# Four feed-forward blocks by a 2x2 block scheme with seven products, in a two-model transformer kernel

## The reference

```python
def _swiglu(x, wg, wu, wd):                    # x (512, 1024); wg, wu (1024, 2816); wd (2816, 1024)
    return (jax.nn.silu(x @ wg) * (x @ wu)) @ wd

for l in range(DEPTH):
    h = 0.5 * _swiglu(x, ffn_w_gate[l, 0], ffn_w_up[l, 0], ffn_w_down[l, 0])
    x = _layernorm(ALPHA * x + h, ln_g[l, 0], ln_b[l, 0])
    h = _mixer(x, ...)
    x = _layernorm(ALPHA * x + h, ln_g[l, 1], ln_b[l, 1])
    h = 0.5 * _swiglu(x, ffn_w_gate[l, 1], ffn_w_up[l, 1], ffn_w_down[l, 1])
    x = _layernorm(ALPHA * x + h, ln_g[l, 2], ln_b[l, 2])
mod = silu(c) @ ada_w + ada_b                  # of the second model, for two vectors c; (1024, 6144)
```

## Time and profile before

| | us |
|---|---|
| median of 3 runs | 3927.68 |
| lowest, highest | 3924.68, 3927.8 |
| span of the profiled execution, first to last instruction | 3922.3 |
| PE busy | 3598.9 (92%) |
| DVE busy | 911.5 (23%) |
| ACT busy | 562.4 (14%) |
| POOL busy | 324.9 (8%) |
| HBM read | 445.96 MB, 115 GB/s over the span |

### The profile page before, as it was taken

How to read it: one execution, slowest core, us unless ns; L and a number is a source line. 1 busy time by engine, 2 the same in 40 slices (tenths; PEclk the granted TensorE clock), 3 DMA queues, 4 the chain that set the end, 5 groups by cost and what they waited for, 6 DMA issues and landing times. The chain is left out here.

```text
span 3922.3 us, 30766 instructions
## 1 busy us (share of the span) xinstructions
PE 3598.9 (92%) x10972; PEld 1711.0 (44%) x10972; DVE 911.5 (23%) x1155; ACT 562.4 (14%) x953; POOL 324.9 (8%) x239
## 2 busy tenths in 40 slices
PE   4999987799999999999589999899897999799998
PEld 2444433434444344444344444374574444343342
DVE  1111017221210211104521210243333300311112
ACT  1000012210000100001310000142353100100001
POOL 1111000011100111000011110100131000100000
PEclk7999998899999999999799999889998999899999
DMA  4333212133332233322023332122211222599996
GB/s 103 97 93 88 75 46 54 33 85 91 96 86 76 73 93 97 80 70 54 22 65 91 96 95 74 53 70 64 80 34 54 75 75 86 214 409 410 410 409 242
DMA packets 533903, 452.63 MB, mean 115 GB/s; under 512 B 32633, under 2 KB 482625, under 8 KB 533585
## 3 DMA queue, kind: packets, MB, share of 16 engines
q1 hardware_dynamic: 533840, 451.78, 36.9%
HBM read 445.96 MB, written 5.77 MB: 115 GB/s over the span
## 5 line engine op out<-in xcount | busy, mean ns | idle before, releaser
L377 PE MATMUL psum<-arena 128*128 128x512 f32 x2816 | 1227.8, 597 | 21.9 <-ACT arena L518 16.3
L377 PEld LDWEIGHTS psum<-arena 128*128 128x128 f32 x2816 | 534.9, 191 | 679.7 <-issue 659.1
L387 PE MATMUL psum<-arena 128*128 128x512 f32 x1408 | 606.5, 591 | 4.8 <-DVE arena L689 4.8
L387 PEld LDWEIGHTS psum<-arena 128*128 128x128 f32 x1408 | 265.7, 189 | 342.7 <-issue 337.5
L1822 PE MATMUL psum<-arena 128*64 128x512 f32 x1536 | 345.8, 600 | 0.8 <-ACT arena L1931 0.8
L689 DVE TENSOR_TENSOR arena<-arena,psum 128x512 f32 x88 | 60.7, 690 | 1005.1 <-ACT arena L525 1005.1
L287 POOL TENSOR_TENSOR arena<-arena 128x1024 f32<-128x1024 f32 x96 | 180.0, 1897 | 1108.0 <-DMA arena<-in_ada_w_dram 1039.1
L1059 PE MATMUL psum<-arena 128*128 128x512 f32 (+1 forms) x576 | 215.1, 534 | 12.2 <-ACT arena L1275 6.4
L1251 PE MATMUL psum<-arena 128*128 128x512 f32 x512 | 220.3, 591 | 0.0
L525 ACT ACTIVATE arena<-psum 128x512 f32<-128x512 f32 x88 | 52.7, 598 | 1119.4 <-PE psum L377 1119.4
L1822 PEld LDWEIGHTS psum<-arena 128*64 128x64 f32 x1536 | 107.0, 137 | 232.5 <-issue 231.5
(11 more groups left out here) (345 smaller groups left out, 2404.7 us busy)
## 6 DMA issues: line engine op xcount, KB each, us to landing
arena<-in_w_gate_dram SPq DMA_DIRECT2D x64, 1024.0 KB, 13.4
arena<-in_w_up_dram SPq DMA_DIRECT2D x64, 1024.0 KB, 14.4
arena<-in_w_down_dram SPq DMA_DIRECT2D x64, 1024.0 KB, 16.8
arena<-in_ffn_w_gate_dram SPq DMA_DIRECT2D x88, 512.0 KB, 4.0
arena<-in_ffn_w_up_dram SPq DMA_DIRECT2D x88, 512.0 KB, 5.3
arena<-in_ffn_w_down_dram SPq DMA_DIRECT2D x64, 704.0 KB, 5.7
arena<-in_w_in_dram SPq DMA_DIRECT2D x144, 256.0 KB, 3.2
arena<-in_ada_w_dram SPq DMA_DIRECT2D x48, 512.0 KB, 5.9
```

The lines of the kernel that those rows point to most:

```text
L377: mm = pe.matmul(bank(side + 2 * half), ring[side][:, c:c + 128], xT[:, k, :], start=(k == 0), stop=(k == KT - 1))
L387: mm = pe.matmul(bank(side), ring[side][:, k * 128:(k + 1) * 128], hid[:, k, :], start=(k == 0), stop=(k == FT - 1))
```

## The change

The four feed-forward blocks cut their matrices into 2x2 blocks: features 0 to 511 and 512 to 1023 (for down, hidden tiles 0 to 10 and 11 to 21), output columns in two halves, tokens 0 to 255 and 256 to 511. Where eight block products stood, seven stand (Winograd's form of Strassen's scheme), with eight sums ahead of them and seven behind.

*Weights.* The ring has four slots of 2048 columns. A slot holds all four blocks of the gate weights, or of the up weights, for hidden tiles i and i + 11. DVE's `sums` makes four block sums of them (two kept beside the weights in `wsum`, one over a block of the slot, one more in `wsum`) and waits for the DMA itself. A pair of units (gate is m = 0, up is m = 1) makes the same two hidden tiles as an iteration before. The down part has 16 units: 4 output pairs q, each in parts of 3, 3, 3 and 2 steps.

*Products.* A step k is seven products with 256 moving columns into seven half banks; set m of four banks belongs to unit m.

*Collecting.* ACT copies the first product to SBUF, DVE adds the rest up (`collect`) and frees the set. Silu runs over both tiles at once. DVE makes four more sums of the hidden tiles, so that `hid` holds seven blocks.

*Activations.* `x_sums` makes four block sums of `xT` for each of four steps. They lie in `rT`'s place, and the norm treats its tiles in the order 0, 4, 1, 5, 2, 6, 3, 7.

*The modulation* keeps its pieces, in other places: DVE reduces column i in pair i, between `collect` of gate and the sums for the next up weights, and PE takes it in the middle of the same pair's unit 1, ahead of its last step. The products of one column go into the unused half of bank 7.

*Layers.* The loop over layers and most small loops are written out. `cpad`, `lpad` and `xc` of the mixer move into `rT`'s place, and the mixer uses the ring of four. POOL adds tiles two by two.

```diff
-        ring = [place(FT * 128) for _ in range(2)]
+        ring = [place(2048) for _ in range(SLOTS)]
+        wsum = [place(3 * 512) for _ in range(2)]
...
+        hid = place(7, HK, HT)
+        blocks = [place(5, HT) for _ in range(2)]
...
+        x_sum = r_flat.rearrange("p (c k h t) -> p c k h t", c=2, k=4, h=2)
+        cpad = r_flat[:, 0:2 * (30 + T)].rearrange("p (a b) -> p a b", a=2)
+        lpad = r_flat[:, 1084:1084 + 2 * (3 + T)].rearrange("p (a b) -> p a b", a=2)
+        xc = r_flat[:, 2114:2114 + 2 * T].rearrange("p (a b) -> p a b", a=2)
...
+        def w_blocks(slot, n):
+            return ring[slot][:, 0:n * 512].rearrange("p (d k f c) -> p d k f c", d=2, f=2, c=128)
+        def w_sums(side, n):
+            return wsum[side][:, 0:n * 384].rearrange("p (s k c) -> p s k c", s=3, c=128)
+        T1, B11, T3, B21, B22, T2, T4 = range(7)
...
+        PARTS = ((0, 3), (3, 3), (6, 3), (9, 2))
+        DOWN = 4 * len(PARTS)
...
+            def up_load(l, s, name, i, g, slot, waits):
+                if waits:
+                    sp.wait_ge(unit_done, g - SLOTS + 1)
+                to = w_blocks(slot, 4).rearrange("p d k f c -> p (d k) f c")
+                for half in range(2):
+                    cols = bass.ds((i + half * UP) * 128, 128)
+                    sp.dma_start(to[:, :, half, :], tiles(d[name][l, s, :, cols])).then_inc(w_ready[slot], 16)
...
+                def pair(i, g, slot, waits):
+                    ada_load(i + f * 12)
+                    up_load(l, s, "ffn_w_gate", i, g, slot % SLOTS, waits)
+                    up_load(l, s, "ffn_w_up", i, g + 1, (slot + 1) % SLOTS, waits)
...
+            def sum_tiles(l, n):
+                for i in range(KT // 2):
+                    if n == 1:
+                        pool.wait_ge(bank_free[0], l * 11 + 7 + i + 1)
+                        pool.wait_ge(bank_free[1], l * 11 + 7 + i + 1)
+                    else:
+                        pool.wait_ge(r_ready, l * 8 + n // 2 * 4 + i + 1)
+                    if i == 0:
+                        pool.tensor_tensor(acc, rT[:, 0, :], rT[:, 1, :], ALU.add)
+                    else:
+                        for k in (2 * i, 2 * i + 1):
+                            pool.drain()
+                            last = pool.tensor_tensor(acc, acc, rT[:, k, :], ALU.add)
+                last.then_inc(acc_ready, 1)
...
+            def products(b0, wv, sv, k, right, first, last):
+                left = ((0, 0, wv[:, 0, k, 0, :], B11), (0, HT, wv[:, 1, k, 0, :], B21),
+                        (3, 0, sv[:, 2, k, :], B22), (1, 0, sv[:, 1, k, :], T2),
+                        (1, HT, wv[:, 1, k, 1, :], T4), (2, 0, sv[:, 0, k, :], T1),
+                        (2, HT, wv[:, 0, k, 1, :], T3))
+                for b, c, w, x in left:
+                    mm = pe.matmul(psum[:, b0 + b, c:c + HT], w, right(x), start=(first and c == 0),
+                                   stop=last, skip_group_check=True)
+                return mm
...
+                pe.wait_ge(ada_ready, a + 2)
+                for w in range(2):
+                    pe.matmul(psum[:, 7, HT + w:HT + w + 1], ada_acc[:, w, :], ones_col,
+                              start=False, stop=True, skip_group_check=True)
...
+            def up_unit(f, b0, slot, k_waits, column):
+                wv, sv = w_blocks(slot, 4), w_sums(b0 // 4, 4)
+                for k in range(4):
+                    if k_waits:
+                        pe.wait_ge(xs_ready, f * 4 + k + 1)
+                    right = {B11: xT[:, k, 0:HT], B21: xT[:, k + 4, 0:HT], B22: xT[:, k + 4, HT:],
+                             T1: x_sum[:, 0, k, 0, :], T3: x_sum[:, 0, k, 1, :],
+                             T2: x_sum[:, 1, k, 0, :], T4: x_sum[:, 1, k, 1, :]}
+                    if k == 3 and column is not None:
+                        ada_column(column)
+                    mm = products(b0, wv, sv, k, right.get, k == 0, k == 3)
+                mm.then_inc(unit_done, 1)
...
+                    for m in range(2):
+                        pe.wait_ge(sums_ready, u + (f * FFN_U + m + 1))
+                        pe.wait_ge(set_free[m], i + (f * 13 + 1))
+                        up_unit(f, 4 * m, (slot + m) % SLOTS, slot == at and m == 0,
+                                i + f * 12 if m else None)
...
+                for u in range(DOWN):
+                    g = at + 2 * UP + u
+                    q, (k0, n) = u // 4, PARTS[u % 4]
+                    pe.wait_ge(sums_ready, f * FFN_U + 2 * UP + u + 1)
+                    if u % 4 == 0:
+                        pe.wait_ge(set_free[q % 2], f * 13 + UP + q // 2 + 1)
+                    wv, sv = w_blocks(g % SLOTS, n), w_sums(u % 2, n)
+                    for k in range(n):
+                        if q == 0:
+                            pe.wait_ge(hid_ready, f * HK + k0 + k + 1)
+                        if q == 1 and k0 + k == HK - 1:
+                            ada_column(f * 12 + UP)
+                        mm = products(4 * (q % 2), wv, sv, k, lambda b: hid[:, b, k0 + k, :],
+                                      k0 + k == 0, k0 + k == HK - 1)
+                    mm.then_inc(unit_done, 1)
...
+                def first_product(m, g):
+                    act.wait_ge(unit_done, g + 1)
+                    act.copy(blocks[m][:, 4, :], psum[:, 4 * m, 0:HT]).then_inc(first_ready, 1)
+                def pair(i, g):
+                    first_product(0, g)
+                    act.wait_ge(set_free[0], i + (f * 13 + 2))
+                    act.activation(blocks[0][:, 0:4, :], blocks[0][:, 0:4, :], ACT.Silu).then_inc(silu_done, 1)
+                    first_product(1, g + 1)
...
+            def x_sums(k, ready):
+                dve.wait_ge(x_ready, ready)
+                lo, hi = xT[:, k, :].rearrange("p (h t) -> p h t", h=2), xT[:, k + 4, :]
+                dve.tensor_tensor(x_sum[:, 0, k, :, :], xT[:, k:k + 5:4, HT:], lo, ALU.subtract)
+                dve.drain()
+                dve.tensor_tensor(x_sum[:, 1, k, 0, :], hi[:, HT:], x_sum[:, 0, k, 0, :], ALU.subtract)
+                dve.drain()
+                dve.tensor_tensor(x_sum[:, 1, k, 1, :], hi[:, 0:HT], x_sum[:, 1, k, 0, :], ALU.subtract)\
+                   .then_inc(xs_ready, 1)
...
+            def sums(side, slot, n, loaded, done):
+                dve.wait_ge(w_ready[slot], loaded)
+                if done is not None:
+                    dve.wait_ge(unit_done, done)
+                wv, sv = w_blocks(slot, n), w_sums(side, n)
+                a11, a12, a21, a22 = wv[:, 0, :, 0, :], wv[:, 1, :, 0, :], wv[:, 0, :, 1, :], wv[:, 1, :, 1, :]
+                dve.tensor_tensor(sv[:, 0, :, :], a21, a22, ALU.add)
+                dve.tensor_tensor(a21, a11, a21, ALU.subtract)
+                dve.drain()
+                dve.tensor_tensor(sv[:, 1, :, :], sv[:, 0, :, :], a11, ALU.subtract)
+                dve.drain()
+                dve.tensor_tensor(sv[:, 2, :, :], a12, sv[:, 1, :, :], ALU.subtract).then_inc(sums_ready, 1)
...
+            def collect(m, ready):
+                ps = psum[:, 4 * m:4 * m + 4, :].rearrange("p b (h t) -> p (b h) t", h=2)
+                out = blocks[m]
+                dve.wait_ge(first_ready, ready)
+                dve.tensor_tensor(out[:, 0:5:4, :], out[:, 4:5, :].to_broadcast([128, 2, HT]), ps[:, 1:3, :],
+                                  ALU.add)
+                dve.drain()
+                dve.tensor_tensor(out[:, 1:4:2, :], out[:, 4:5, :].to_broadcast([128, 2, HT]), ps[:, 4:6, :],
+                                  ALU.add)
+                dve.drain()
+                dve.tensor_tensor(out[:, 1, :], out[:, 1, :], ps[:, 6, :], ALU.add)
+                dve.tensor_tensor(out[:, 2:4, :], out[:, 3:4, :].to_broadcast([128, 2, HT]), ps[:, 3:5, :],
+                                  ALU.add).then_inc(set_free[m], 1)
...
+                def pair(i, slot, g, loaded, last):
+                    for m in range(2):
+                        if last:
+                            n = at + 2 * UP + m
+                            sums(m, n % SLOTS, PARTS[m][1], landed(n), g + (m + 1))
+                        else:
+                            sums(m, (slot + 2 + m) % SLOTS, 4, loaded[m], g + (m + 1))
+                        if m:
+                            put_modulation(i + f * 12)
+                        collect(m, i * 2 + (f * 26 + m + 1))
+                        if m == 0:
+                            ada_reduce(i + f * 12)
+                    dve.drain()
+                    dve.wait_ge(silu_done, i + (f * UP + 1))
+                    h = bass.ds(i, 1)
+                    four = hid[:, B11:B11 + 4, h, :].rearrange("p b o t -> p b (o t)")
+                    dve.tensor_tensor(four, blocks[0][:, 0:4, :], blocks[1][:, 0:4, :], ALU.mult)
+                    dve.drain()
+                    def at_tile(b, n=1, step=1):
+                        return hid[:, b:b + (n - 1) * step + 1:step, h, :].rearrange("p b o t -> p b (o t)")
```

(57 more changed lines are left out.)

350 lines of the change are left out of this document (157 added, 193 removed).

## The result

| | before | after |
|---|---|---|
| median, us | 3927.74 (4 runs) | 3755.3 (4 runs) |
| lowest, highest | 3924.68, 3928.72 | 3754.56, 3756.02 |
| span of the profiled execution | 3922.3 | 3754.0 |
| mean granted clock of TensorE | 0.954 | 0.947 |
| HBM read | 445.96 MB | 445.96 MB |

What follows compares the result with a forecast made beforehand. PE's own work was taken as the bound. Blocks 1 to 3 at -42.8 each (-128.4), block 0 -41.3, norms +5.8 gave -164: span 3922.3 to 3758, plus 5.4 for the median, 3764 us; range 3725 to 3850.

Steps and rivals of the forecast that it cites:

- Record spacing 0.2168 us, from line 1181: PE's products of 256 columns with own weight load: 0.2168 us a record, read from 32 such records in 7.10 us.
- The rival in which loads don't hide: PE's block products: 7392 records at 0.403 us instead of 0.2168, +1376 us, 5140 us in all; chance 0.01.
- The wait in the pair, 0.4 us: Up loop, unit 1: PE waits for DVE's reduction, 9.54 us against 9.11 of PE's products, 0.4 us paid every pair.
- DVE keeps up behind unit 1, 3.3 us left: Up loop: DVE's 8.8 us of work after unit 1 fits beside unit 0's 12.14 us of PE, costing nothing.
- The chain over POOL and SP to the weights, hidden: Up loop: reduction, POOL's products, SP's loads; first weights at 20 us of the pair, wanted at 25.05, hidden by 5 us.
- Down, -19.3 a block: Down part of each block: 616 records in 133.5 us against 151.62 + 1.21 before, a saving of 19.3 us.
- End of a block, +5.0: From a block's last product to the mean: 7.4 us with the drain, against 2.43 before, +5.0 us.
- The start, +3.0: Start of a block, from the scaling to PE's first product: 4.5 us against 1.57 before, +3.0 us.
- The mixer's norm, +1.4: In the mixer's norm POOL adds two tiles behind the last instead of one: +1.4 us, two times.
- The lock of DVE and POOL, +1.0 in each of three norms: In three norms DVE's weight sums beside POOL's additions lock each other out, +1.0 us each.
- The first start, +4.5: First block: sums of up (2.77) and first x sums (1.55) stand behind the up weights' landing at 64.38, +4.5 us.
- the prediction's clause that a wait of this length brings the lower clock: In the DVE-bound rival (chance 0.05): after a 2.69 us wait two records took 2.08 us, the level of 1.2 GHz.

Runs made afterwards that it cites:

- third edit: Against the changed kernel, in three norms the second unit's weight sums moved behind the subtractions, out of POOL's way; 3747.62 us, ratio to before 0.9542.

## Why the prediction was right, step by step

- **Record spacing 0.2168 us, from line 1181: right.** 24.68 - 0.37 over 112 records is 0.2171, with seven half banks in turn, where line 1181 stays in one half bank for 16 records. The rival in which loads don't hide is gone: a load lasts 190 ns and stands wholly inside the spacing. The trace disagrees here with the row-group rule of the Trainium skill (TensorE: Matmul & The Clock Gate, The mechanism), which would give 0.403. The same section also says that a load for a background weight buffer is pulled ahead of matmuls in flight, and with that the rows would agree; the prediction weighed the rule alone.
- **The wait in the pair, 0.4 us: the mechanism right, the size too large.** It measured 0.18. DVE's 8.94 us ahead of the reduction's end were 8.92, but the three hand-overs of 0.20 were not all there: the one to ACT's copy and back lay beside the sums, and PE's column starts 0.05 us after the reduction's end. PE's 9.11 us were right, so the difference was nearly nothing. The pair was -3.05, not -2.86, and 44 x 0.19 makes 8.4 us of the forecast's error.
- **DVE keeps up behind unit 1, 3.3 us left: right.** 3.09 measured, and adding 2.3 us of work there cost nothing.
- **The chain over POOL and SP to the weights, hidden: right.** DVE never waits for a weight DMA in the loop, though a gate half lands 6.2 us after its issue, not 4.0.
- **Down, -19.3 a block: right.** From the last up column (1052.47) to ACT's first copy behind the last record (1189.55) are 137.1 us; less two columns (0.37 each) and 14 records of up (3.04) that is 133.3, where 133.5 were forecast, and the idle time of line 409 shows no gap at the entry or behind it.
- **End of a block, +5.0: 7.20 us measured, which is +4.5.** The term took 7.4 us from PE's last product and 2.43 from DVE's start; from the same mark, before was 2.69, and the sum would have had +4.7. The start, +3.0: 4.49 us against 1.57, +2.9. The mixer's norm, +1.4: 4.17 against 2.77.
- **The lock of DVE and POOL, +1.0 in each of three norms: right in kind, about right in size.** 0.56 us of additional wait at the one end of a block; 0.49 in the mixer's norm, and 0.6 more until DVE's subtractions start. The Trainium skill's statement on it (SBUF — State Buffer, SBUF: two separate sides) agrees with the rows of 1.60 to 2.39 us for operations of 0.69.
- **The first start, +4.5: mis-sized, +7.9 measured.** The term took 64.38, when the up weights landed before, as the time from which the sums count. Before, 1 MB had to land for it; now both halves of the gate and of the up weights, 2 MB, which were there at 67.6, and only then came the sums of up and of `xT`.
- **Not in the sum: 3.2 us at the norms, the mixers and the second model** (6.6 in all, as below, less 3.4 at the first start). The second model is 2.3 us longer with the same code, the mixer of layer 1 takes 4.0 more where 1.4 and a part of the lock stood, the other one 0.5. Part of it is clock: the mean's two records ahead of that mixer took 1.12 us and take 2.07 now, and the first 98 records of the second block took 23.58 us, those of the third 22.86. A longer wait alone doesn't decide it: before, the same two records took 2.08 us behind a wait of 2.69 and 1.12 behind one of 2.77, so the prediction's clause that a wait of this length brings the lower clock rested on one of two rows that differ. In the second model the rows show clock as well, in both directions: at one place ten records took 4.56 us before (3297.99, granted clock 1.00), and six of the same take 4.52 now (3129.71, 0.50), which is 1.7 us.
- **DVE busy about 1630: 1607.5.** Operations without a drain between them overlap at their ends (869.54 to 870.15 is 0.61 us for one of 0.69), where the sum counted each in full.

Block by block: first product to the mean, the sum had -31.5 - 19.3 + 5.0 = -45.8 and the mean of the four is -48.6; outside, it had 4.5 + 9.0 + 5.8 = +19.3 and +25.9 was measured. So -164 was -168.3, and two errors of opposite sign hide in the 4 us: -11 in the pairs and at the ends of the blocks, +6.6 at the first start and elsewhere. That they nearly cancel is luck. The 5.4 us added for the median, where 1.3 were measured, put the forecast 4.1 us higher still.

## What to carry to other kernels

Where one engine is busy without gaps, the price of taking work from it can be read from one row that has the new form of its instruction, and the rest of the change is one question: at which place is the helping engine late? Here the same three DVE operations cost 120 us at one place of the loop and nothing at another; so the slack of each place has to be worked out by itself, since DVE's busy share (43%) tells neither. The reduction, which only must be done once per iteration, was cheapest where DVE idled anyway, even though it made DVE collide there with POOL. And an edit's worth is read in the stretch that it touches: of the third edit's 7.7 us, 3.2 lay in code that it didn't touch.

## What was not expected of the hardware

- A wait of 2.15 us in every pair left the clock alone in most pairs and halved it for about 3 us in others (0.50 from 836.60 to 839.60 in a pair of 28.79 us, 1.00 from 880.00 to 907.00), in the same loop with the same wait. In which pairs it comes is open.
- Where DVE sums of two SBUF operands run beside POOL's products, two operations of 0.69 us take 2.39 and 2.23, where the worst row of before had 1.680, while POOL loses 0.82 us on 3.75.
- The gate halves took 6.2 us to land instead of 4.0 with the same bytes, and SP took 3.46 us to issue the two DMAs of an up load in the pair shown above, and up to 4.8 elsewhere, where it took 0.53 us for the one DMA of an up load before. In the loop nothing waited for either.
